# A hybrid encoder layer: the output projection by seven block products, with the merged sums sent through DRAM

## The reference, cut to what matters

```
gates = jax.nn.sigmoid(gate_in.reshape(B, T, N_BRANCH, D))
merged = jnp.sum(gates * jnp.einsum('btiw,iwd->btid', branches, w_branch[l]), axis=2)
x = x + jnp.einsum('btd,de->bte', merged, w_out[l])
return rmsnorm(x, final_norm_g)
```

## Time and profile before

| | |
|---|---|
| Median of 3 runs | 3310.61 us (3310.06 to 3316.44) |
| The profiled execution's own time | 3311.61 us |
| Its span, first to last instruction | 3309.8 us |
| PE busy in the span | 3236.8 us (98%) |
| DVE, ACT, POOL busy | 2017.3, 1328.2, 1081.1 us |
| Units and outputs of the last stage | about 2749 to 3299 us of the span |
| Mean granted clock of TensorE | 0.995 of full speed |

### The profile page before, as it was taken

How to read it: one execution, slowest core, us unless ns; L and a number is a source line. 1 busy time by engine, 2 the same in 40 slices (tenths; PEclk the granted TensorE clock), 3 DMA queues, 4 the chain that set the end, 5 groups by cost and what they waited for, 6 DMA issues and landing times. The chain is left out here.

```text
span 3309.8 us, 51014 instructions
## 1 busy us (share of the span) xinstructions
PE 3236.8 (98%) x19052; PEld 2542.0 (77%) x19052; DVE 2017.3 (61%) x4622; ACT 1328.2 (40%) x2170; POOL 1081.1 (33%) x491
## 2 busy tenths in 40 slices
PE   8999999999999999999999997999999999999998
PEld 6888888887888888888877774666666667888887
DVE  3322312225676667666758778888888668556654
ACT  3111111114344434443433336677777665223421
POOL 3322313243333333333333324555555443000000
PEclk9999999999999999999999999999999999999999
DMA  6545445466454544544448975221221358667562
GB/s 226 188 160 189 155 156 186 160 205 214 134 197 141 170 158 147 191 142 135 146 152 280 338 235 159 67 77 39 79 76 44 115 210 291 232 208 248 176 218 71
DMA packets 319014, 555.63 MB, mean 168 GB/s; under 512 B 35694, under 2 KB 115438, under 8 KB 318768
## 3 DMA queue, kind: packets, MB, share of 16 engines
q1 hardware_dynamic: 267296, 471.66, 43.7%
q10 hardware_dynamic: 51472, 80.71, 6.6%
HBM read 382.43 MB, written 169.82 MB: 167 GB/s over the span
## 5 line engine op out<-in xcount | busy, mean ns | idle before, releaser
L785 POOL TENSOR_TENSOR glaf_w_lo<-early_raw,glaf_w_hi 128x1024 fp32r<-128x1024 f32 x140 | 343.5, 2454 | 613.6 <-ACT glaf_w_hi L759 612.0
L814 PE MATMUL glaf_dense_acc<-h_hi,glaf_w_hi 128*128 128x512 f32 x1120 | 449.1, 401 | 1.4 <-POOL glaf_w_lo L785 1.0
L814 PE MATMUL glaf_dense_acc<-h_lo,glaf_w_hi 128*128 128x512 f32 x1120 | 437.6, 391 | 0.0
L814 PE MATMUL glaf_dense_acc<-h_hi,glaf_w_lo 128*128 128x512 f32 x1120 | 435.6, 390 | 0.0
L1851 DVE CUSTOM_DVE_ANT_0 front_p<-diff_s_ps,ahead_table 128x512 f32<-128x512 f32 x544 | 346.8, 686 | 66.0 <-PE diff_s_ps L1705 63.0
L559 POOL TENSOR_TENSOR proj_w_lo<-early_raw,proj_w_hi 128x1024 fp32r<-128x1024 f32 x84 | 202.8, 2415 | 477.3 <-DVE proj_w_hi L509 477.3
L1788 ACT ACTIVATE front_p<-front_p,diff_neg_max 128x2048 f32<-128x2048 f32 (+1 forms) x160 | 278.7, 1742 | 7.6 <-DVE diff_neg_max L1859 7.6
L1729 PE MATMUL diff_oT_ps<-diff_aT,diff_v 128*128 128x512 f32 x544 | 272.6, 602 | 7.6 <-ACT diff_aT L1781 7.6
L219 PE MATMUL proj_acc<-h_hi,proj_w_hi 128*128 128x512 f32 x672 | 263.0, 391 | 0.6 <-POOL proj_w_lo L559 0.6
L221 PE MATMUL proj_acc<-h_hi,proj_w_lo 128*128 128x512 f32 x672 | 261.7, 389 | 0.0
L220 PE MATMUL proj_acc<-h_lo,proj_w_hi 128*128 128x512 f32 x672 | 261.5, 389 | 0.0
(11 more groups left out here) (221 smaller groups left out, 7116.6 us busy)
## 6 DMA issues: line engine op xcount, KB each, us to landing
early_raw<-in_w_zg SPq DMA_DIRECT2D x180, 512.0 KB, 4.4
early_raw<-in_w_stream SPq DMA_DIRECT2D x80, 512.0 KB, 3.6
scratch_zg<-glaf_dense_out SPq DMA_DIRECT2D x140, 256.0 KB, 2.2
items_raw<-in_w_br SPq DMA_DIRECT2D x120, 256.0 KB, 2.8
merge_gate<-scratch_zg SPq DMA_DIRECT2D x120, 256.0 KB, 3.3
scratch_featT<-proj_out ACTq DMA_DIRECT2D x80, 256.0 KB, 2.4
items_br_hi<-scratch_item_hi SPq DMA_DIRECT2D x60, 256.0 KB, 5.8
items_br_lo<-scratch_item_lo SPq DMA_DIRECT2D x60, 256.0 KB, 7.0
```

The source lines that it names most:

```text
L785: pool.tensor_tensor(self.w_lo[:, s], self.raw[:, u % self.RAW], self.w_hi[:, s], ALU.subtract).then_inc(self.lo_split, 1)
L814: done = pe.matmul(self.acc[:, u % self.banks], a, x, start=i == 0, stop=i == self.PER - 1)
```

## The change

The stage is cut in two. `phase_branches` runs all 120 units of the five chunks. Each finished sum is stored to a DRAM tensor `meT` in fp32 (`store_sum`, 256 KB after every third unit), and no longer split in SBUF. The gate buffers go from six to four. `phase_outputs` follows and does the output projection of ten pairs of token tiles (256 tokens by 1024 channels).

A pair is seen as a 2 by 2 matrix of blocks: the rows are the two token tiles, the columns the two halves of the channels. The weights are 2 by 2 blocks as well. Where the plain product needs eight block products (96 matmuls), the new one forms seven (84 matmuls) from sums and differences of blocks. On the weight side (`Output`) GpSimd makes four sums for each of four steps `kt`, ACT the seven high parts and GpSimd the seven low parts, within the first 45 units. On the token side, for each pair: GpSimd makes four sums (`sums`, 128x512 each), ACT seven high parts (`high`), DVE seven low parts (`low`). Of the seven products PE makes, ACT copies the first to `s1`; DVE adds the others, seven additions of 128x512, and GpSimd adds `s1`, `u2` and `u3` to the quadrants of `x`, four additions of 128x512. Square, inverse root and scaling then go for both tiles of the pair. Twelve slots hold the parts, two buffers (`me`) the sums read back from DRAM, two hold `x`.

The diff, cut to what the text below speaks of:

```diff
--- before.py
+++ after.py
@@ -56,6 +56,11 @@
...
+FORMS = 7
+B11, T2, B21, T3, T1, T4, B22 = range(FORMS)
+A11, S2, A12, S3, S1, A22, S4 = range(FORMS)
+
+
+class Output:
...
+    HALF, STAGE, GATES = KT // 2, 2, 4
...
+        self.me = [low[:, at * kb:(at + 8) * kb].rearrange("p (k t) -> p k t", k=KT) for at in (14, 0)]
...
+    def load(self, sp, kt):
+        if kt:
+            sp.wait_ge(self.low, FORMS * kt)
+        for half in range(self.STAGE):
+            sp.dma_start(self.stage[:, half], self.w_o[:, half * self.HALF + kt]).then_inc(self.wo_in[half], 16)
...
+    def combine(self, pool, kt):
+        step = Chain(pool, self.sums, 4 * kt)
+        for half in range(self.STAGE):
+            pool.wait_ge(self.wo_in[half], 16 * (kt + 1))
+        t1, t2, t3, t4 = (self.source(kt, form) for form in (T1, T2, T3, T4))
+        step(pool.tensor_tensor(t1, self.block(0, 1), self.block(0, 0), ALU.subtract))
+        step(pool.tensor_tensor(t3, self.block(1, 1), self.block(0, 1), ALU.subtract))
+        step(pool.tensor_tensor(t2, self.block(1, 1), t1, ALU.subtract))
+        step(pool.tensor_tensor(t4, self.block(1, 0), t2, ALU.subtract))
+
...
+    def split_low(self, pool, n):
+        kt, i = divmod(n, FORMS)
+        form = self.order[i]
+        pool.wait_ge(self.high, n + 1)
+        pool.tensor_tensor(self.lo[:, form, kt], self.source(kt, form), self.hi[:, form, kt], ALU.subtract).then_inc(self.low, 1)
+
...
+def phase_branches(nc, used, shared, items, output, zg, meT, item_hi, item_lo, w_br, cross):
...
+        RING, RAW, WS, GS = 4, Items.RAW, Items.SLOTS, Output.GATES
...
+            def store_sum(c, d):
+                n = c * KT + d
+                sp.wait_ge(combined, (n + 1) * NB)
+                sp.dma_start(meT[d, :, c * CH:(c + 1) * CH], total[:, n % 2]).then_inc(me_stored[n % 2], 16)
...
+                    if r % NB == NB - 1:
+                        store_sum(c, r // NB)
+                    for kt in range(1, Output.HALF):
+                        if u == WO_FIRST + WO_PER * kt - 1:
+                            output.load(sp, kt)
                     if c == 0 and PER - r == NB:
...
+                    if c == NC - 1 and r == PER // 2:
+                        sp.wait_ge(output.low, WO_ALL)
+                        for b in range(2):
+                            sp.wait_ge(me_stored[b], 16 * (KT // 2))
+                        sp.dma_start(output.me[0], meT[:, :, 0:2 * P].rearrange("k p t -> p k t")).then_inc(me_first, 16)
...
+            for u in range(UNITS):
...
-            def outputs(c):
...
-            for c in range(NC):
-                for r in range(PER):
-                    branch(c * PER + r)
-                outputs(c)
...
+def phase_outputs(nc, used, shared, output, x_all, meT, final_gain, y, branches):
...
+        def wait_for_slot(engine, i, form):
+            n = FORMS * i + form
+            if n < RING:
+                engine.wait_ge(branches.unit_done, branches.units)
+            else:
+                engine.wait_ge(prod_done, n - RING + 1)
...
+        @block.sync
+        def _(sp):
+            def load_x(i):
+                if i >= XS:
+                    sp.wait_ge(y_out[i % XS], 32 * (i // XS))
+                for t in range(2):
+                    sp.dma_start(x[:, i % XS, t], rows(x_all, (2 * i + t) * P, P)).then_inc(x_in[i % XS], 16)
+
+            def load_me(i):
+                if i >= 2:
+                    sp.wait_ge(form_low, FORMS * (i - 2) + A22 + 1)
+                    sp.wait_ge(s_steps, 4 * (i - 2) + 4)
+                sp.dma_start(me[i % 2], meT[:, :, 2 * i * P:2 * (i + 1) * P].rearrange("k p t -> p k t")).then_inc(me_in[i % 2], 16)
+
+            def store_y(i):
+                for t in range(2):
+                    sp.wait_ge(normed, 2 * i + t + 1)
+                    sp.dma_start(rows(y, (2 * i + t) * P, P), x[:, i % XS, t]).then_inc(y_out[i % XS], 16)
+
+            sp.wait_ge(branches.unit_done, branches.units)
+            load_x(0)
+            sp.wait_ge(branches.combined, branches.units)
+            sp.dma_start(gain, final_gain).then_inc(gain_in, 16)
+            for semaphore, value in branches.stores:
+                sp.wait_ge(semaphore, value)
+            load_me(1)
+            load_x(1)
+            for i in range(PAIRS):
+                if i:
+                    store_y(i - 1)
+                if i and i + 1 < PAIRS:
+                    load_x(i + 1)
+                if i + 2 < PAIRS:
+                    load_me(i + 2)
+            store_y(PAIRS - 1)
+            for b in range(XS):
+                sp.wait_ge(y_out[b], 32 * (PAIRS // XS))
+
...
+            def high(i, form):
+                if form == A11:
+                    wait_for_me(act, i)
+                wait_for_slot(act, i, form)
+                if form in (S2, S3, S1, S4):
+                    act.wait_ge(s_steps, 4 * i + {S3: 1, S2: 2, S1: 3, S4: 4}[form])
+                act.activation(f_hi[:, slot(i, form)], source(i, form), ACT.Copy).then_inc(form_high, 1)
+
...
+                act.activation(s1[:, :], bank(i, A11), ACT.Copy).then_inc(s1_ready, 1)
+
+            for form in range(FORMS):
+                high(0, form)
+            for i in range(PAIRS):
+                if i:
+                    act.wait_ge(squared, 2 * i - 1)
+                    square(i - 1, 0)
+                if i + 1 < PAIRS:
+                    high(i + 1, A11)
+                first_product(i)
+                if i + 1 < PAIRS:
+                    for form in range(1, FORMS):
+                        high(i + 1, form)
+                if i:
+                    act.wait_ge(squared, 2 * i)
+                square(i, 1)
+            act.wait_ge(squared, 2 * PAIRS - 1)
+            square(PAIRS - 1, 0)
...
+            for i in range(PAIRS):
+                if i + 1 < PAIRS:
+                    for which in (S3, S2, S1):
+                        sums(i + 1, which)
+                pool.wait_ge(x_in[i % XS], 32 * (i // XS + 1))
+                pool.wait_ge(s1_ready, i + 1)
+                add(i, 0, 0, s1[:, :])
+                if i + 1 < PAIRS:
+                    sums(i + 1, S4)
+                pool.wait_ge(out_added, ADDS * i + U2_DONE)
+                add(i, 0, 1, u2[:, :])
+                pool.wait_ge(out_added, ADDS * i + U3_DONE)
+                add(i, 1, 1, u3[:, :])
+                add(i, 1, 0, u3[:, :])
...
+        @block.tensor
+        def _(pe):
+            pe.wait_ge(output.low, FORMS * HALF)
+            for i in range(PAIRS):
+                for form in range(FORMS):
+                    wait_for_bank(pe, i, form)
+                    pe.wait_ge(form_low, FORMS * i + form + 1)
+                    g = slot(i, form)
+                    for k in range(HALF):
+                        done = product3(pe, bank(i, form), f_hi[:, g, k], f_lo[:, g, k], output.hi[:, form, k], output.lo[:, form, k], k == 0, k == HALF - 1)
+                    done.then_inc(prod_done, 1)
...
+            def low(i, form):
+                dve.wait_ge(form_high, FORMS * i + form + 1)
+                if form in (S2, S3):
+                    dve.wait_ge(s_steps, 4 * i + 4)
+                dve.tensor_tensor(f_lo[:, slot(i, form)], source(i, form), f_hi[:, slot(i, form)], ALU.subtract).then_inc(form_low, 1)
...
+            for i in range(PAIRS):
+                more = i + 1 < PAIRS
+                if more:
+                    low(i + 1, A11)
+                if i:
+                    inverse(i - 1)
+                if i:
+                    dve.wait_ge(x_added, SHARES * (i - 1) + X12_ADDED)
+                dve.wait_ge(s1_ready, i + 1)
+                add(u2[:, :], i, S2, s1[:, :])
+                if i:
+                    scale(i - 1)
+                if more:
+                    low(i + 1, S2)
+                dve.wait_ge(x_added, SHARES * i + X11_ADDED)
+                add_to(i, A12, 0, 0)
+                if i:
+                    dve.wait_ge(x_added, SHARES * (i - 1) + X21_ADDED)
+                dve.wait_ge(out_added, ADDS * i + U2_DONE)
+                add(u3[:, :], i, S3, u2[:, :])
+                if more:
+                    low(i + 1, A12)
+                    low(i + 1, S3)
+                dve.wait_ge(x_added, SHARES * i + X22_ADDED)
+                add_to(i, S1, 1, 1)
+                dve.wait_ge(x_added, SHARES * i + X12_ADDED)
+                add_to(i, S1, 0, 1)
+                if more:
+                    low(i + 1, S1)
+                    low(i + 1, A22)
+                dve.wait_ge(x_added, SHARES * i + X21_ADDED)
+                add_to(i, A22, 1, 0)
+                if more:
+                    low(i + 1, S4)
+                dve.wait_ge(out_added, ADDS * i + C12_BEGUN)
+                add_to(i, S4, 0, 1)
+            inverse(PAIRS - 1)
+            scale(PAIRS - 1)
...
```

343 lines of the change are left out of this document (186 added, 157 removed).

## The result

The changed kernel takes 3388.19 us in the median of four runs (3383.15 to 3390.65); the kernel before took 3311.05 beside it. The ratio is 1.0227, with an interval of 1.0214 to 1.0239: slower by 77 us, inside the range and in its upper part. The profiled execution has a span of 3387.4 us at a mean granted clock of 0.987, against 3309.8 before, so the two traces show the same 77.6 us.

What follows compares the result with a forecast made beforehand. PE, busy 98% of the span, was taken as the bound. Matmuls -27.2, reload +56, clock +6, entry +3.2, pair loop +17 and rest +0.8 sum to +55.8 us: forecast 3366 us, range 3336 to 3392.

Steps and rivals of the forecast that it cites:

- the pair loop with the tail: Output phase: loading and scaling through DRAM outlasts PE's 19.1 us a pair, +17 us (0 to 31); end of kernel, +0.8.
- chunks 0 and 1: Chunk 0: shorter queue before item stores against more GpSimd work beside DVE, put at 0 us, between -4 and +6.
- the entry: Start of the output phase: PE waits 2.3 us for first parts, more at its second product; +3.2 us (2 to 6).
- Reload and clock: Four changes of chunk: units 0 to 2 wait for item loads, +56 us (48 to 64); slowed PE clock, +6.
- the fallen clock: After waits at changes of chunk PE runs at half clock: 1.5 us each, +6 us in all (0 to 12).
- the rival of a free loop: Output phase: the pairs' feeding loop, 17.6 us against PE's 19.1, does not bind; 3349 us, chance 0.25.
- A turn: One round of the pairs' feeding loop: 17.6 us, with GpSimd and DVE holding each other 20.2 to 22.6; 21.8 used.
- Two of my own signs of being wrong: Wrong if PE idles under 8 us per change of chunk, or the ten pairs take under 194 or above 225 us.
- Both bind harder: Rival: pair turn of 24 us (+14), clock at upper bound (+6), chunk 0 at +5; 3391 us, chance 0.17.
- The covered reload: Rival at the four changes of chunk: item loads stay hidden, only saved matmuls show; 3287 us, faster, chance 0.04.

Runs made afterwards that it cites:

- e1: Changed kernel without the 24 item loads at each of the four changes of chunk, so later chunks read chunk 0's tiles: 3331.23 us, 1.0060.
- e6: Changed kernel with GpSimd's sums and additions in the output phase cut to one column, roundings reading plain tiles: 3356.03 us, 1.0133.
- e10: Changed kernel without item loads of chunks 1 to 4, GpSimd's output-phase and output-weight work cut to one column: 3292.19 us, 0.9940.
- e12: Changed kernel reloading only the high half of each item tile at the four changes of chunk: 3358.38 us, 1.0138.
- e3: Changed kernel with SP issuing the load of the sums of pair i+2 ahead of y stores and x loads: 3370.00 us, 1.0174.

## Why the prediction was right, and where its sizes were off

**Direction, mechanism and place were right.** What bounded before was PE, fed from a queue that was full for 20 us per chunk behind work that the change moved away. The forecast of 3366 us is 22 us under the result, and 17.5 of the 22 are one term, the pair loop with the tail. The other 4 to 5 are chunks 0 and 1 (6.4), the entry (0.7) and a reload that was 2.5 cheaper.

**Reload and clock: 62 forecast, 59.5 by matmul starts, 57 by e1.** The three later changes of chunk took 13.4 to 14.3 us for 13.2 + 1.5, the first 18.3 for 17.4. The issue times and landings of the kernel before could be carried over as they stood. Within the 62 the split was off. The last tile landed 25.0, 21.0, 20.2 and 20.6 us after E, the end of the chunk's last unit, and unit 2 ended 1.5, 1.5, 1.3 and 1.1 us after that. 0.7 of each are the three matmuls that were left, so the fallen clock cost 0.4 to 0.8 us a change, 2.7 in all for the 6 of the forecast, and the reload itself 56.8 for 56. At half clock PE ran for longer (5.6 to 6.0 us of slow time a change), but mostly while it would have waited. Rows 7 were also misread in part: after the wait that ended at 2774.16 the matmuls were slow (0.62) from 2775.19 on, 1 us later and not 2.

**The mis-sized term is the feeding loop of the pairs: +17.8 forecast with the tail, 35.3 measured.** That is above its own upper bound (31 for the loop, 0.8 for the tail). The mechanism was the predicted one, and the rival of a free loop (3349) fell. The size came out of these places:

- A turn took 23.4 us on average (the first scalings start at 3185.45, the eighth at 3349.51, seven turns lie between), where I took 21.8: +11.5. The part on the queue, from the end of the scalings to the landing of the sums, took 10.2 to 11.7 us in the seven turns, 11.0 on average, for my 10.6 (the turn shown is the longest: 3258.52 to 3270.21). That is some 3 us of the 11.5. From issue to landing the nine loads of the sums took what the first row below says.
- The part of ACT and DVE, from the landing to the end of the scalings, took 12.4 to 12.5 us in every one of the seven turns (3270.21 to 3282.66 in the one shown). With all five GpSimd instructions ready my working had 12.0, with three 9.6, and I took 11.2. In the turn shown all five stood in a row beside the root, so the upper end was the right one. This is the other 9 us, and e6 shows whose they are.
- The first scalings ended at E+41.9 and not at E+36: +5.9. In e6 they end at E+32.0, so GpSimd's part before them is 10 us.
- From the eighth scalings to the last addition it took 22.3 us for 23: -0.7.

```profile
DMA to landing us min/median/max: 6.7/7.8/8.3
```

```profile
3270.32 1.30 POOL L2668 TENSOR_TENSOR outs_form_full<-output_low 128x512 f32<-128x512 f32 x1 [6.59 <-DMA output_low<-scratch_meT]
...
3276.05 1.26 POOL L2674 TENSOR_TENSOR outs_form_full<-output_low,outs_form_full 128x512 f32<-128x512 f32 x1
```

So the last addition ended 228 us after the last unit and not 212 (0.7 of it the longer entry). From there to the end it took 12.1 us for 9.2 before, where I forecast 0.8 more: +2.1. Two squares and two stores stand there now, not one.

**Two of my own signs of being wrong came up.** I had written that the prediction is wrong if the ten pairs take above 225 us where I count 212. Counted in that way, from the last unit to the last addition, they took 228. So by this sign the size of the pair term was wrong, though the time stayed in the range. The other was PE's idle time under 8 us at each change of chunk. It was 12.3, 8.7, 7.8 and 7.5 us, so under 8 at two of the four; another 5.6 to 6.0 us at each were slow time, and only the two together, 13.4 to 18.3 us, are what reload and clock cost.

**Chunks 0 and 1: 0 forecast between -4 and +6, measured +6.4.** Just past the bound. I had looked at GpSimd and at the bytes, not at ACT, whose order now meets three 1 MB loads one unit after their issue (21.2 us of ACT's time; read from the trace of e10).

**Entry: 3.2 forecast, 3.9 measured**, inside 2 to 6, but not for the reason given. I had 2.3 us for the first product and 0.9 for a wait at the second. The first product alone took 3.9, since GpSimd's first sums already held DVE: its last addition took 1.14 us and its first low part 1.74 in place of 0.69 and 0.68, and in e6 PE starts after 2.4. At the second product the trace has no wait, as the first ran at half clock. That the sum came near is luck.

**Rivals.** "Both bind harder" (3391, chance 0.17) came nearer to the time than the forecast, 3 us against 22. Of its three parts the turn of 24 us and chunk 0 at +5 came about (23.4 and +6.4), the clock at its upper bound did not. The covered reload (3287) is excluded by e1 and e12.

## What to carry to other kernels

A saving on the engine that bounds is worth only what its cover is not: before taking work away, list which transfers and waits lie under it, with issue and landing times, and price them as if they were bare. For a loop through DRAM and several engines, walk it link by link in the trace, take the landing time of each transfer as it stands behind others and not its bytes, and where two engines hold each other up, take the worse order. And when a loop is cut, look for the next one under it: in e3 it was 20.8 us a turn, 2.6 us shorter than the first.

## What the runs showed of the hardware that was not expected

Instructions of DVE with a single tile as input are held up by GpSimd too. `TENSOR_SCALAR` on 128x2 took 1250 ns (fp32, L2726) and 1147 ns (int32, L204) while GpSimd worked on 128x512, and 162 and 169 ns in e6. Such a step lasts until GpSimd's instruction is done: the one that began at 3272.09 ended at 3273.34, and the sum that GpSimd began at 3271.70 ended at 3273.32. I had counted nine of the twelve root steps as exposed, not these. The Trainium skill allows for it: on the page SBUF — State Buffer (Who interferes with whom), copy, cast and tensor_scalar can enter a mode that takes the pair of ports shared with GpSimd, and then contend. The trace agrees with that as far as it shows a hold. Which conditions decide no run here shows.

The holding up goes both ways, and shows on the side of GpSimd as well: its 128x512 additions into `x` take 1.3 us at the least, 1.7 beside low parts, and 1.9 to 2.3 where they meet a scaling (spans on GpSimd are rough):

```profile
3254.98 3.51 DVE L2733 SCALAR_TENSOR_TENSOR outs_x<-outs_x,output_stat,output_low 128x1024 f32<-128x1024 f32 x2
3255.49 1.91 POOL L2677 TENSOR_TENSOR outs_x<-outs_x,outs_u 128x512 f32<-128x512 f32 x1 [2.35 <-DVE outs_u L2718]
```

Two scalings took 3.51 us, for 2.48 in the last pair, where GpSimd was done.
